# Order of the weight split and the key search at the start of two expert layers, in a one-core RWKV-7 / latent-attention / PEER step

## The reference, cut to what matters

```python
q = (xb @ w_q).reshape(PEER_BLOCK, PEER_HEADS, 2, PEER_D_KEY // 2)   # 8 heads, 2 halves of 128
s = jnp.einsum('thcd,cnd->thcn', q, sub_keys).astype(F32)            # 128 keys for each half
s1, i1 = lax.top_k(s[:, :, 0], PEER_TOPK)                            # 16 best of each half
s2, i2 = lax.top_k(s[:, :, 1], PEER_TOPK)
cand_s = s1[..., :, None] + s2[..., None, :]                         # 256 pairs
top_s, top_pos = lax.top_k(cand_s, PEER_TOPK)                        # 16 best pairs
gate = jax.nn.softmax(top_s, axis=-1)
act = jax.nn.gelu(jnp.einsum('thkd,td->thk', u_tab[experts], xb).astype(F32))
return jnp.einsum('thk,thkd->td', (gate * act).astype(xb.dtype), v_tab[experts])
```

## Time and profile before

| | us |
|---|---|
| median of 3 runs | 3045.79 |
| the runs | 3033.13, 3048.67, 3045.79 |
| profiled execution, own time | 3036.44 |
| its span, first to last instruction | 3034.8 |
| TensorE matmul busy in the span | 2768.0 (91%) |
| VectorE busy | 1833.6 (60%) |
| ScalarE busy | 1261.5 (42%) |
| mean granted TensorE clock, share of full speed | 0.938 |

### The profile page before, as it was taken

How to read it: one execution, slowest core, us unless ns; L and a number is a source line. 1 busy time by engine, 2 the same in 40 slices (tenths; PEclk the granted TensorE clock), 3 DMA queues, 4 the chain that set the end, 5 groups by cost and what they waited for, 6 DMA issues and landing times.

```text
span 3034.8 us, 60374 instructions
## 1 busy us (share of the span) xinstructions
PE 2768.0 (91%) x22131; PEld 2522.1 (83%) x22131; DVE 1833.6 (60%) x3435; ACT 1261.5 (42%) x2565; POOL 181.6 (6%) x248
## 2 busy tenths in 40 slices
PE   8988699999999999975699999947999999999998
PEld 5777589999999999953488888822899999999998
DVE  5566457989985555525334444450579899855554
ACT  2333014467764444411233434410134677644443
POOL 0054000000000000000011111112000000000000
PEclk9999599999999999996689999975999999999999
DMA  4310034444445555530011122134345444455554
GB/s 163 120 43 27 15 119 152 162 163 157 160 148 181 182 182 180 205 144 0 1 42 57 57 58 58 57 89 135 121 150 167 160 154 160 148 182 182 181 180 139
DMA packets 112530, 378.00 MB, mean 125 GB/s; under 512 B 14617, under 2 KB 24090, under 8 KB 111842
## 3 DMA queue, kind: packets, MB, share of 16 engines
q1 hardware_dynamic: 88562, 322.17, 31.9%
q0 software_dynamic: 13424, 43.98, 4.9%
q10 hardware_dynamic: 10368, 9.44, 1.0%
HBM read 371.52 MB, written 4.01 MB: 124 GB/s over the span
## 4 chain that ended last, share of the span: by engine, by line
PE 87%; DVE 6%; issue 2%; ACT 2%; ACTq 1%; DMA 1%; DVEq 0%; POOLq 0%; POOL 0%; SPq 0%
PE ps L714 85%; DVE arena L1285 2%; ACT arena L1935 1%; DVE arena L1289 1%; ACTq L541 1%; DMA arena<-in_cache_n 1%; PE ps L1013 1%; PE ps L1008 1%; ACTq L542 0%; DVE ring_lo L1285 0%; PE ps L773 0%; DVE arena L1799 0%; ACT w_hi L1935 0%; DMA ring<-in_wstream 0%; DVE arena L1802 0%
## 5 line engine op out<-in xcount | busy, mean ns | idle before, releaser
L1285 DVE TENSOR_TENSOR ring_lo<-ring,w_hi 128x1024 fp32r<-128x1024 f32 x512 | 625.5, 1224 | 416.7 <-ACT w_hi L1935 413.3
L1935 ACT ACTIVATE arena<-ps 128x256 f32<-128x256 f32 (+19 forms) x981 | 397.5, 425 | 904.2 <-PE ps L714 823.5
L1935 ACT ACTIVATE w_hi<-ring 128x1024 fp32r<-128x1024 f32 x512 | 541.8, 1059 | 389.0 <-PE ps L714 388.6
L714 PE MATMUL ps<-arena 64*64 64x64 f32 (+11 forms) x5228 | 500.1, 275 | 143.4 <-DVEq L1282 54.6
L714 PE MATMUL ps<-x_hi,w_hi 128*128 128x264 f32 x2048 | 596.7, 291 | 15.5 <-DVE ring_lo L1285 15.5
L714 PEld LDWEIGHTS ps<-arena 64*64 64x64 f32 (+6 forms) x5228 | 391.5, 159 | 254.0 <-DMA arena<-in_cache_n 57.2
L714 PE MATMUL ps<-h_hi,w_hi 128*128 128x264 f32 x2048 | 580.1, 283 | 6.8 <-DVE ring_lo L1285 6.8
L714 PE MATMUL ps<-x_hi,ring_lo 128*128 128x264 f32 x2048 | 586.3, 286 | 0.0
L714 PE MATMUL ps<-x_lo,w_hi 128*128 128x264 f32 x2048 | 586.0, 286 | 0.0
L714 PE MATMUL ps<-h_lo,w_hi 128*128 128x264 f32 x2048 | 582.3, 284 | 0.0
L714 PE MATMUL ps<-h_hi,ring_lo 128*128 128x264 f32 x2048 | 581.9, 284 | 0.0
(11 more groups left out here) (158 smaller groups left out, 2296.4 us busy)
## 6 DMA issues: line engine op xcount, KB each, us to landing
ring<-in_wstream SPq DMA_DIRECT2D x608, 512.0 KB, 3.3
arena<-in_cache_t POOLq DMA_DIRECT2D x128, 192.0 KB, 2.6
arena<-in_cache_n ACTq DMA_DIRECT2D x72, 128.0 KB, 2.4
arena<-in_cache_n POOLq DMA_DIRECT2D x56, 128.0 KB, 2.7
arena<-in_mla_w POOLq DMA_DIRECT2D x1, 3072.0 KB, 10.3
arena<-in_state POOLq DMA_DIRECT2D x4, 512.0 KB, 4.8
out_wkv_s<-arena POOLq DMA_DIRECT2D x4, 512.0 KB, 5.2
arena<-in_consts SPq DMA_DIRECT2D x1, 1408.0 KB
```

Of the source, the lines that this page charges most:

```text
L714: return nc.tensor.matmul(out, lhsT, rhs, start=start, stop=stop, **kw)
L1285: return v.tensor_tensor(out, a, b, op)
L1935: return nc.scalar.activation(out, in_, func, **kw)
```

## The change

Three edits. The three first upper halves are made in ScalarE's query loop, behind steps 13, 14 and 15, and no longer behind the loop (the definition of `upper` is moved up for this). On VectorE the three first lower halves and the paced ones start at head 7 (PH - 1) in place of head 4 (PH // 2). The exponentials stand ahead of tile 16 in place of tile 38.

```diff
-EXP_AT = 38
+EXP_AT = 16
...
                 for h in range(PH):
                     w.next(s_copied, 2)
-                    if h == PH // 2:
+                    if h == PH - 1:
                         pace(WHI * PACE)
-                    choose_head(h, pace if h >= PH // 2 else no_pace)
+                    choose_head(h, pace if h == PH - 1 else no_pace)
                 w.next(s_copied)
...
                         tell(bank_free[b], s_copied)
+                    if 16 - WHI <= g < 16:
+                        upper(g - (16 - WHI))
                 w.next(for_act)
...
-                for e in range(WHI):
-                    upper(e)
                 for n in range(LEAD_U):
                     if n == EXP_AT:
```

More of the change, by code:

```diff
@@ L1963, in peer, with upper @@
                 fn(x_hi[:, :], xnbuf).then_inc(xhi_ready, 1)
+                u0 = TILES[f"peer{layer}"]
+                def upper(e, it=0):
+                    n = u0 + e
+                    act.wait_ge(slot_in[n % RING], it * 48 + 16 * (n // RING + 1))
+                    if e >= WHI:
+                        act.wait_ge(tile_used, it * 15 + (n - WHI + 1))
+                    fn(upper_of(e), slot(n).rearrange("p c m -> p (c m)")).then_inc(hi_ready, 1)
                 for g in range(17):
@@ L1977, in peer @@
                 tell(bank_free[3], s_copied)
-                u0 = TILES[f"peer{layer}"]
                 s0, p0 = NSETS * layer, (P - LEAD_U) * layer
                 done = marks["done", layer]
[L1982 to L1988, removed]
                 def gelu(n):
```

## The result

The changed kernel takes 3062.7 us (median of 12 runs, 3058.0 to 3072.0), the kernel before 3039.2 in the same comparison (12 runs, 3026.6 to 3048.7). The ratio is 1.008, with a 95% interval of 1.0066 to 1.0094: 24 us slower (20 to 29). The forecast was 20.8 us slower. The stated 3066 rested on a median of before, 3045.79, that a longer series puts 6.6 us lower.

A forecast was written before the change was run, and what follows sets the result against it. TensorE, 87% of the last-ending chain, was taken as the bound, so its start and gaps count. Layer delays of 9.9 and 10.9 us gave +20.8 us on the 3045.79 median: 3066.6, stated as 3066, range 3050 to 3077.

The forecast's parts named there:

- Start: TensorE's first expert matmul, behind seven heads on VectorE: 16.8 us later in each layer.
- Uppers in the loop: Three upper copies in ScalarE's query loop: cost 0, and the move alone gains nothing.
- Restart: TensorE's first expert tiles after idling run at half clock: 2.5 us lost per layer, bounds 1.9 to 3.9.
- Exponentials and choices: TensorE's waits at tiles 39 and 46: 4.58 us plus 2.0 of half clock, and 0.91 us, go.
- the detour: ScalarE's table load, exponentials and load back at tile 16: 3.2 us on ScalarE, cost 0.
- Unpaced end: Gates' last operations without a lower half, at half 29 or 30: stall 0 to 2.3 us, 1.0 taken per layer.
- Sum: Tile 46's transposes later by 9.9 us in layer 0 and 10.9 in layer 1: +20.8 us.
- Absorbed: Rival: VectorE's surplus buys back waits behind tile 46, leaving +11 us, 3057 on the median; chance 0.18.
- the waits come back: Rival: gate tail or table detour makes TensorE wait over 3 us, clock falls: +29 us, 3075; chance 0.10.
- the heads run faster: Rival: VectorE's heads between 464 and 494 us take under 10.20 us each, so not slower; chance 0.07.

The follow-up runs named there:

- e2: Changed kernel with six heads ahead of the first lower half, not seven, and exponentials at tile 22: +6 us (2 to 11) against the kernel before.
- e3: Changed kernel with five heads ahead of the first lower half, not seven, and exponentials at tile 28: -17 us (-22 to -12) against the kernel before.
- e1: Changed kernel with the three first upper copies back behind ScalarE's query loop: +22 us (17 to 28) against the kernel before.
- e5: Kernel before with only the three first upper copies moved into the query loop: -6 us (-11 to -1) against the kernel before.
- e9: Changed kernel with 156 extra matmuls filling TensorE's wait ahead of the first expert tile: +18 us (12 to 24) against the kernel before.
- e8: Kernel before with upper copies in the query loop and exponentials at tile 32, still four heads ahead: -16 us (-22 to -10) against the kernel before.
- e4: Kernel before with only the exponentials moved, to tile 32 from 38: -7 us (-12 to -1) against the kernel before.
- e10: Changed kernel with two lower halves issued among the sample operations ending the gates: +22 us (14 to 29) against the kernel before.
- e6: Changed kernel with 140 extra matmuls in TensorE's wait ahead of the first expert tile: +26 us (19 to 33) against the kernel before.
- e7: Changed kernel with five heads ahead, exponentials at tile 28, two lower halves among the gates' last sample operations: -20 us (-27 to -14) against the kernel before.

## Why the prediction was right

The sum forecast +20.8 us and the stages show +24.1: sign, place and mechanism were right, and its terms came out as follows. That the stated 3066 us lies within 3.4 us of the measured 3062.7 is in part luck: the median of before was 6.6 us too high and the sum 3.3 us too low. The terms' own bounds (restart 1.9 to 3.9, tail 0 to 2.3) also give +17.6 to +26.2 and not the +15 to +27 written down.

- **Start.** Predicted 16.8 us later per layer. Measured: 87.1 - (478.94 - 408.73) = 16.9 in layer 0, 87.1 - 70.1 = 17.0 in layer 1. e2 and e3 take it back in steps of one head. It is the term that decided the sign.
- **Uppers in the loop.** Costed at nothing; e1 confirms it, and ScalarE stood 0.19 us ahead of the copy at 463.93, for its own work and not for a ring slot. The sentence that the move gains nothing held for this kernel alone: e5 shows 4 to 5 us per layer where VectorE wants the halves at once.
- **Restart.** Taken as 2.5; e9 measures 2.7. The reading that a gap over 3 us is paid twice, as wait and as half clock, was too simple: in e8 one of 1.9 us was, and in the kernel before the one of 3.42 us ahead of the first output tile wasn't.
- **Exponentials and choices.** 4.58 of wait and its 2.0 of half clock went, and the 0.91 at the choices too. "Cost 0" for the detour was a little off: two waits, 0.48 and 0.30 us, follow it. They come as was reckoned for the gates' end: a VectorE operation of 2.29 us (from 553.71) is still running when the upper half comes (555.26), and the lower half starts only behind it (555.92). With the exponentials at tile 32 (e4, e8) TensorE has no such wait. The drain of 1.38 us per switch that the Trainium skill gives (ScalarE: Activation LUTs, What ACT_TABLE_LOAD costs) isn't seen here either: in the changed kernel the detour takes from 543.63 to 546.86, 3.2 us for two loads and three exponentials, with 0.02 us or less between one and the next.
- **Unpaced end.** Predicted 0 to 2.3, taken with the above as 1.0; 1.4 us of waits stood there in all. e10 shows the 0.64 to be its part and worth 0.9.
- **Sum.** +9.9 and +10.9 predicted, +11.5 and +12.6 measured. From the first expert matmul to the mark it was to be 138.2 us and was 139.8. Of the 1.6 us missing, the waits' brackets are 0.4 and the restart 0.2. Most of the remaining 1 us hangs on the waits too: each delays TensorE by some 0.25 us more than its bracket says. Around the third wait of the changed kernel two successive `gelu` operations start 3.80 us apart, 0.89 more than the 2.91 of an undisturbed tile, for a bracket of 0.64:

```profile
581.41 0.39 ACT L1935 ACTIVATE arena<-ps 128x264 f32<-128x264 f32 x1 [1.57 <-PE ps L714]
585.21 0.39 ACT L1935 ACTIVATE arena<-ps 128x264 f32<-128x264 f32 x1 [2.47 <-PE ps L714]
```

  At the other two it is 3.64 and 3.45 us, so the three waits cost 2.2 us and not 1.4, and 0.9 is what e10 gained by one of them. e9, with a full clock, has the same (635.41 - 498.36 = 137.1, where 46 x 2.91 + 1.4 + 0.7 is 136.0). That the last 0.25 us belongs to the wait at the start in the same way is an inference.
- **Rivals.** "Absorbed" fails on 278.7 against 278.6 us behind the mark; "the waits come back" on a longest of 0.64; "the heads run faster" on VectorE's heads at 10.2 us, the last ones beside an idle TensorE too (474.90 to 485.10 between two heads' same operation, both in the chain above).

## What to carry to other kernels

When two kinds of work share an engine, look first at which of them another engine waits for: work pulled ahead of it costs its full length once the cover ends, here the query loop, which is five heads long and not seven. A wait that hangs on a tile's number (the exponentials at 38) is taken away by moving that number alone, and making an input early pays only where its reader stands waiting for it (e5 against e1). Compare single stages between two marks in the trace when the effect is near the scatter of whole runs, and put the second mark far enough behind: the half clock that a wait leaves can begin after it, as in e8.

## What the runs showed of the hardware that was not expected

How long TensorE stood didn't settle alone whether its granted clock fell, when, or for how long. In the expert stages of these profiles no gap of 0.3 to 1.1 us was followed by half clock (1.08 in e9 among them). Of gaps of 1.9 us, those in e8 were, in both layers, and those in e4 were not, with the same operations on TensorE around them. Gaps of 3.0 to 3.2 us always were, but in some cases only 1.3 us or more after the matmuls had begun again (before in layer 1, e6 in layer 1, e4), and TensorE then worked at half clock for 3.4 us in place of the some 6 us behind 20 us of idling. That is the 1.2 us by which the stage of the kernel before was shorter in layer 1 (214.2) than in layer 0 (215.4). The gap of 3.42 us ahead of the first output tile shows all three courses: of 24 cases, two layers in twelve profiles, the clock stayed at 1.00 in three (before, e5 in layer 0), averaged 0.62 or 0.63 over the next 8 us in three (e1 in layer 0, e5 and e7 in layer 1) and 0.79 to 0.81 in the others. What decides between the courses was not tried.

The programs also differ in these profiles where they should agree, ahead of the compared stages. The first query matmul stands at 408.73 us before, 405.56 after, 399.62 in e2 and 416.58 in e1, though all programs are the same up to there; from the mark of layer 0 to the queries of layer 1 it is 1533.1 (e5) to 1544.4 us (e1). The granted clock in 340 to 380 us differs as well (0.64 before, 0.66 after, 0.83 in e2, 0.63 in e1). Whether the clock is the cause was not tried.
